# Recurrent layer: head outputs with tokens on partitions, normed by a root for each token, and turned on PE behind the turns of k and v

## What is computed

```python
def hgrn2_mixer(x, w_in, w_out, norm_g, lb):
    H, K, V, C = HGRN_HEADS, HGRN_DK, HGRN_DV, HGRN_CHUNK      # 8, 128, 128, 64
    q_raw, f_raw, i_raw = jnp.split(x @ w_in, [H * K, 2 * H * K], axis=-1)
    log_f = jnp.logaddexp(jnp.log(lb), jnp.log1p(-lb) + jax.nn.log_sigmoid(z))      # z = f_raw
    key, q, v = (1.0 - lb) * jax.nn.sigmoid(-z), jax.nn.silu(q_raw), i_raw
    b = jnp.cumsum(log_f, axis=3)                              # within a chunk
    q_dec, k_dec = q * jnp.exp(b), key * jnp.exp(-b)
    a = jnp.where(causal, jnp.einsum('bhcid,bhcjd->bhcij', q_dec, k_dec), 0.0)
    o_intra = jnp.einsum('bhcij,bhcje->bhcie', a, v)
    # states: the running sum of keys times values, decayed from chunk to chunk
    o = o_intra + jnp.einsum('bhcid,cbhde->bhcie', q_dec, states)
    o = o * lax.rsqrt(jnp.mean(o * o, axis=-1, keepdims=True) + RMS_EPS) * norm_g   # per head and token
    return o.reshape(B, S, H * V) @ w_out
```

## Time and profile before

| | |
|---|---|
| median of 3 runs | 2247.62 us (2245.55 to 2248.52) |
| the profiled execution | 2243.69 us, its span 2241.9 us |
| PE busy | 2137.8 us, 95% of the span |
| DVE busy | 1280.1 us, 57% |
| ACT busy | 886.7 us, 40% |
| mean granted clock of PE | 0.968 of full speed |
| chain that ended last | PE 81%, DVE 11%, DVEq 4%, ACT 2% |

### The profile page before, as it was taken

One profiled execution on the slowest core, in us unless ns is written; L12 is line 12 of the kernel. 1 busy time (PEld: TensorE's weight loads), 2 busy tenths in 40 slices (PEclk: granted clock), 3 DMA queues, 4 the chain that ended last, 5 costly groups with the idle time before them and its releaser, 6 DMA issues.

```text
span 2241.9 us, 29415 instructions
## 1 busy us (share of the span) xinstructions
PE 2137.8 (95%) x11002; PEld 1741.6 (78%) x11002; DVE 1280.1 (57%) x2043; ACT 886.7 (40%) x1298; POOL 69.3 (3%) x63
## 2 busy tenths in 40 slices
PE   7969999999999999999988999999999998999997
PEld 5757778888877888888877788888777876888886
DVE  6987454434454666666676642344568886433444
ACT  4225232222227556566552431242345524322322
POOL 1000300000130000000000000000000000000000
PEclk8988999999999999999999899999999998999998
DMA  4102222232232212212221223222112221222221
GB/s 168 30 10 78 93 75 94 86 114 100 71 117 85 85 59 74 85 66 70 80 76 52 76 97 109 94 94 94 57 58 75 75 76 67 102 94 94 94 96 55
DMA packets 31518, 183.46 MB, mean 82 GB/s; under 512 B 5184, under 2 KB 5568, under 8 KB 12736
## 3 DMA queue, kind: packets, MB, share of 16 engines
q1 hardware_dynamic: 27504, 176.18, 23.1%
q10 hardware_dynamic: 3024, 6.00, 0.8%
q0 software_dynamic: 896, 0.06, 0.0%
HBM read 180.06 MB, written 2.10 MB: 81 GB/s over the span
## 4 chain that ended last, share of the span: by engine, by line
PE 81%; DVE 11%; DVEq 4%; ACT 2%; issue 1%; DMA 1%; ACTq 0%
PE ps L569 12%; PE ps L571 12%; PE ps L570 12%; PE ps L1058 6%; PE ps L1060 5%; PE ps L1059 5%; PE ps L1114 2%; PE ps L1115 2%; PE ps L1116 2%; PE ps L630 1%; PE ps L620 1%; PE ps L599 1%; PE ps L625 1%; PE ps L969 1%; DVE f_run L2608 1%
## 5 line engine op out<-in xcount | busy, mean ns | idle before, releaser
L1284 ACT ACTIVATE w_hi<-raw 128x2048 fp32r<-128x2048 f32 (+1 forms) x122 | 226.0, 1853 | 297.1 <-PE ps L571 220.2
L569 PE MATMUL ps<-x_hi,w_lo 128*128 128x512 f32 x816 | 317.6, 389 | 0.5 <-DVE y L2205 0.3
L571 PE MATMUL ps<-x_hi,w_hi 128*128 128x512 f32 x816 | 317.5, 389 | 0.0
L570 PE MATMUL ps<-x_lo,w_hi 128*128 128x512 f32 x816 | 317.4, 389 | 0.0
L1725 DVE TENSOR_TENSOR w_lo<-raw,w_hi 128x2048 fp32r<-128x2048 f32 (+3 forms) x116 | 259.3, 2235 | 93.1 <-ACT w_hi L1284 92.6
L1058 PE MATMUL ps<-x_hi,w_lo 128*128 128x512 f32 x544 | 218.8, 402 | 2.9 <-DVE w_lo L2375 2.4
L1060 PE MATMUL ps<-x_hi,w_hi 128*128 128x512 f32 x544 | 213.1, 392 | 0.0
L1059 PE MATMUL ps<-x_lo,w_hi 128*128 128x512 f32 x544 | 212.5, 391 | 0.0
L569 PEld LDWEIGHTS ps<-x_hi,w_lo 128*128 128x128 f32 x816 | 153.2, 188 | 32.9 <-issue 0.7
L570 PEld LDWEIGHTS ps<-x_lo,w_hi 128*128 128x128 f32 x816 | 153.2, 188 | 31.9
L571 PEld LDWEIGHTS ps<-x_hi,w_hi 128*128 128x128 f32 x816 | 153.2, 188 | 31.8
(11 more groups left out here) (453 smaller groups left out, 3966.5 us busy)
## 6 DMA issues: line engine op xcount, KB each, us to landing
raw<-w_attn_in SPq DMA_DIRECT2D x32, 1024.0 KB, 5.0
raw<-w_gate_up SPq DMA_DIRECT2D x22, 1024.0 KB, 4.9
raw<-w_up_a SPq DMA_DIRECT2D x16, 1024.0 KB, 4.9
raw<-w_down_a SPq DMA_DIRECT2D x16, 1024.0 KB, 4.9
raw<-w_up_h SPq DMA_DIRECT2D x16, 1024.0 KB, 5.0
raw<-w_down_h SPq DMA_DIRECT2D x16, 1024.0 KB, 4.9
raw<-w_hgrn_in SPq DMA_DIRECT2D x8, 1024.0 KB, 4.9
raw<-w_down SPq DMA_DIRECT2D x8, 768.0 KB, 4.3
```

The source lines that it names most:

```text
L569: pe.matmul(o, w_lo[:, slot, a:a + P], hi[:, k, :], start=k == 0, stop=False)
L570: pe.matmul(o, w_hi[:, slot, a:a + P], lo[:, k, :], start=False, stop=False)
L571: last = pe.matmul(o, w_hi[:, slot, a:a + P], hi[:, k, :], start=False, stop=k == st.kc - 1)
L1284: act.activation(w_hi[:, slot, 0:width], raw[:, slot, 0:width], ACT.Copy).then_inc(whi_ready, 1)
```

## The change

- PE: L1200 and L1208 swap their operands, so that the head's output has tokens on the partitions: four blocks of 128 tokens by 128 features in bank 7, for head 7 too (`O_LAST` goes). The state's part writes one half of the partitions at a time, 64 tokens of a chunk. L1216 goes. New is `turn_head`: four transposes of the scaled output `hg_tok` into bank 5, for head `hd - 2`, behind the turns of k and v; the one of head 7 stands at the end, before the last chunk of the output projection.
- ACT: four squares of 128 columns, each of which also sums over its columns (`accum_out`), give the sum for each token; the root is one of 128x4. The high part `xo_hi` is read from bank 5 with the gain as scale. In step 8 an early root of one element loads the table for it.
- DVE: `scale_head` takes a reciprocal of 128x4 and scales bank 7 into `hg_tok` (128x512), in all steps with an `attend`, at the end of the step. The low part `xo_lo` is read from bank 5 too, with the gain in it.
- The key-value products of head `a` wait for the low part of head `a - 1`, since bank 5 holds its turned output, and no longer for the root.

```diff
             def step(hd, par, project, attend):
 
                 a, old = hd - 1, 1 - par
-                o_bank = O_BANK if project else O_LAST
...
+                if not (isinstance(hd, int) and hd < 2):
+                    turn_head(hd - 2)
                 if project:
                     hgrn_tile(hd, par, 1, range(DC))
                 else:
                     out_part(0, range(4, 5))
                 if attend:
                     pe.wait_ge(ht_ready, a + 1)
-                    pe.wait_ge(root_ready, SK["head0"] + a)
+                    if not first(a):
+                        pe.wait_ge(xlo_ready, XB["hgrn_out"] + a)
...
-                        pe.matmul(ps[:, o_bank, sl], v_htok[:, b, :], tmp[:, 3, sl], start=b == 0, stop=False,
+                        pe.matmul(ps[:, O_BANK, sl], tmp[:, 3, sl], v_htok[:, b, :], start=b == 0, stop=False,
...
-                        sl = slice(c * CHUNK, (c + 1) * CHUNK)
-                        last = pe.matmul(ps[:, o_bank, sl], state[:, c, :], q_dec[:, old, sl], start=False, stop=c == 7,
-                                         skip_group_check=True)
+                        half, at_ = CHUNK * (c % 2), (c // 2) * P
+                        last = pe.matmul(ps[half:half + CHUNK, O_BANK, at_:at_ + P], q_dec[:, old, c * CHUNK:(c + 1) * CHUNK],
+                                         state[:, c, :], start=False, stop=c >= 6, skip_group_check=True)
...
-                    pe.wait_ge(sq_ready, SB["head0"] + a + 1)
-                    pe.matmul(ps[:, 5, :], ones, sq[:, 0, :], start=True, stop=True).then_inc(sq_used, 1)
+
+            def turn_head(n):
+
+                pe.wait_ge(oh_ready, n + 1)
+                for b in range(TB):
+                    last = pe.transpose(ps[:, 5, b * P:(b + 1) * P], hg_tok[:, b, :], ident)
+                last.then_inc(oht_done, 1)
...
             step(HG_HEADS, 0, False, True)
             out_part(1, range(3, 6))
-            out_part(0, range(6, DC))
-            out_part(1, range(6, DC))
-            pe.wait_ge(oh_ready, HG_HEADS)
+            out_part(0, range(6, DC - 1))
+            out_part(1, range(6, DC - 1))
+            turn_head(HG_HEADS - 1)
+            out_part(0, range(DC - 1, DC))
+            out_part(1, range(DC - 1, DC))
...
                 if attend:
                     act.wait_ge(oh_done, a + 1)
-                    act.activation(sq[:, 0, :], ps[:, SUM if project else O_LAST, :], ACT.Square).then_inc(sq_ready, 1)
+                    for b in range(TB):
+                        act.activation(sq[:, 0, b * P:(b + 1) * P], ps[:, SUM, b * P:(b + 1) * P], ACT.Square,
+                                       accum_out=mean4[:, b:b + 1])
...
-                    act.wait_ge(sq_used, SB["head0"] + a + 1)
+                    act.drain()
                     act.wait_ge(rstd_ready, SK_ROOT["head0"] + a)
-                    act.activation(root[:, :], ps[:, 5, :], ACT.Sqrt, bias=eps[:, 0:1], scale=1.0 / P) \
-                       .then_inc(root_ready, 1)
+                    act.activation(root4, mean4, ACT.Sqrt, bias=eps[:, 0:1], scale=1.0 / P).then_inc(root_ready, 1)
...
-            def finish(a, bank):
+            def scale_head(a):
                 dve.wait_ge(root_ready, SK["head0"] + a + 1)
-                dve.reciprocal(rstd[:, :], root[:, :]).then_inc(rstd_ready, 1)
-                settle()
-                stt(chunk(hg_o, a), ps[:, bank, :], gains[:, ds(GAIN_AT["g_hgrn"] + a, 1)], rstd[:, :], ALU.mult,
-                    ALU.mult).then_inc(oh_ready, 1)
+                dve.reciprocal(rstd4, root4).then_inc(rstd_ready, 1)
+                settle()
+                tt(hg_tok[:, :, :], ps[:, SUM, :].rearrange("p (b f) -> p b f", b=TB),
+                   rstd4.unsqueeze(2).to_broadcast([P, TB, P]), ALU.mult).then_inc(oh_ready, 1)
```

More of the change, by code:

```diff
@@ L189, in build @@
     f_start = at("f_start", Y_AT + 2 * KB, [T])
+    hg_tok = at("hg_tok", Y_AT + 4 * KB, [TB, P])
     k_tok = at("k_tok", Y_AT + 12 * KB, [TB, P])
@@ L291, in build @@
         SUMS += [("mean_" + part, 0), ("var_" + part, 8)]
-    SUMS += [(f"head{n}", 1) for n in range(HG_HEADS)]
+    SUMS += [(f"head{n}", 0) for n in range(HG_HEADS)]
     for part in ("mix_h", "ffn_h"):
@@ L393, in build @@
     oh_done, oh_ready = sem("oh_done"), sem("oh_ready")
+    oht_done = sem("oht_done")
     out_done = sem("out_done")
@@ L1195, in step @@
                         out_part(1, range(0, 2))
-                    elif not (isinstance(a, int) and a == 0):
+                    if not first(a):
                         pe.wait_ge(oh_ready, a)
@@ L1679, in step @@
                        .then_inc(ht_ready, 1)
-                if project and not (isinstance(hd, int) and hd < 2):
+                if not (isinstance(hd, int) and hd < 2):
                     head_hi(hd - 2)
@@ L1687, in step @@
                         split_next(hd, par, i, 1)
+                if not project:
+                    act.activation(sq[:, 1, 0:1], eps[:, 0:1], ACT.Sqrt)
                 if attend:
                     act.wait_ge(oh_done, a + 1)
-                    act.activation(sq[:, 0, :], ps[:, SUM if project else O_LAST, :], ACT.Square).then_inc(sq_ready, 1)
+                    for b in range(TB):
+                        act.activation(sq[:, 0, b * P:(b + 1) * P], ps[:, SUM, b * P:(b + 1) * P], ACT.Square,
+                                       accum_out=mean4[:, b:b + 1])
                 if project:
@@ L1694, in step @@
                 if attend:
-                    act.wait_ge(sq_used, SB["head0"] + a + 1)
+                    act.drain()
                     act.wait_ge(rstd_ready, SK_ROOT["head0"] + a)
-                    act.activation(root[:, :], ps[:, 5, :], ACT.Sqrt, bias=eps[:, 0:1], scale=1.0 / P) \
-                       .then_inc(root_ready, 1)
+                    act.activation(root4, mean4, ACT.Sqrt, bias=eps[:, 0:1], scale=1.0 / P).then_inc(root_ready, 1)
             def head_hi(hd):
-                act.wait_ge(oh_ready, hd + 1)
-                act.activation(chunk(xo_hi, hd), chunk(hg_o, hd), ACT.Copy).then_inc(xhi_ready, 1)
+                act.wait_ge(oht_done, hd + 1)
+                act.activation(chunk(xo_hi, hd), ps[:, 5, :], ACT.Copy, scale=gains[:, ds(GAIN_AT["g_hgrn"] + hd, 1)]) \
+                   .then_inc(xhi_ready, 1)
             step(0, 0, 0, True, False)
@@ L1710, in _ @@
             step(HG_HEADS, 0, 0, False, True)
-            head_hi(HG_HEADS - 2)
             head_hi(HG_HEADS - 1)
@@ L2611, in step @@
                     stt(k_dec[:, par, :], hg_k[:, par, :], rest_, f_run[:, :], ALU.mult, ALU.mult).then_inc(dec_ready, 1)
-                if attend and project and not (isinstance(hd, int) and hd == HG_HEADS - 1):
-                    finish(a, SUM)
+                if attend:
+                    scale_head(a)
             step(0, 0, True, False)
```

9 lines of the change are left out of this document (2 added, 7 removed).

## The result

The changed kernel takes 2250.29 us (median of 20 runs, 2247.64 to 2253.66), the kernel before, run beside it, 2245.82 (20 runs, 2238.16 to 2249.13): ratio 1.0023, interval 1.0015 to 1.0031, so 5.2 us slower (3.4 to 7.0) on that median. The profiled execution of the changed kernel took 2250.28 with a span of 2248.5.

What follows compares the result with a forecast made beforehand. The prediction took the recurrent layer's steps as bound by DVE from kv products to k_dec and by PE from there back. Turns +3.0 and end +1.7 made +4.7 us, 2247.6 to 2252.3; range 2248.5 to 2261.

Steps and rivals of the forecast that it cites:

- Two sections with different owners: recurrent layer's step: DVE owns kv products to k_dec, 16.0 us; PE owns k_dec to kv products, 7.5; other's work hidden.
- ones matmul: L1216 on PE, between kv products and k_dec: removal frees 1.0 us a step, worth nothing where DVE is late.
- the shorter passes: L1208's 14 passes on PE, between kv products and k_dec: 1.48 us become 1.0, the saving hidden in the steps.
- The turns: four transposes on PE between k_dec and kv products, steps 2 to 7: 0.5 us each step, +3.0 us.
- The four squarings: ACT's summing squares of 128 columns: at most 3.3 us, making ACT at most 2.7 later, covered.
- rival 4: turns wait for the scaling because the root is late: from 2253 us upward, chance 0.04.
- The reciprocal: on DVE between k_dec and kv products: 3.35 us becomes 0.17, worth nothing as DVE already waits there.
- DVE's slack ahead of the kv products: DVE's total wait for the key-value products in the stage: from 21.3 us to about 45.
- The end: step 8 and the stage's end, where PE's order decides: +1.7 us, bounds 0.5 to 3.3.
- the bound by PE: rival: PE's work bounds the steps, so the kernel gets faster, 2241.8 us; chance 0.07, 0.04 more for a milder form.
- The end that costs nothing: rival: step 8's kv products and the weights' split don't wait; only the turns cost, 2250.3 us, chance 0.13.
- The fall of the clock: rival: PE's clock drops in the longer wait at the scores; two falls 2255.7 us, all seven 2264.2, chance 0.22.

Runs made afterwards that it cites:

- run 1: the changed kernel with the head's four turns of steps 2 to 7 moved behind the kv products: 2248.1 us, ratio 1.0011 to the kernel before.
- run 9: the changed kernel with head 7's turns earlier and the end's chunks in the order of the kernel before: 2246.9 us, ratio 1.0001.
- runs 2 and 3: the changed kernel with unread turns of v added in steps 1 to 8: eight behind the kv products (ratio 1.0015), or four behind the scores (1.0033).
- run 7: the changed kernel with DVE splitting the next weights' low part twice in steps 1 to 7, for longer PE waits: 2275.0 us, ratio 1.0121.
- run 10: the changed kernel with kv products three chunks early, head 7's turns early, v's copy before the squarings, end chunks in before's order: 2236.8 us, ratio 0.9965.
- run 6: the kernel before with the kv products put ahead of the last two chunks of tile 1: 2240.7 us, ratio 0.9973.

## Why the prediction was right

**Two sections with different owners.** This carried the forecast, and runs 1 to 3 show it. The 1.0 us of the ones matmul and the shorter passes (1706.73 - 1705.71 = 1.02, forecast 1.0) moved nothing, and reappear as PE's wait at the scores: 2.6 to 11.2 us, forecast 13. The wait is 1.72 a step, forecast 1.8 to 1.9.

**The turns, +3.0 forecast, +2.2 measured.** Right in place, off in size. They take 0.44 us, with nothing for a wait in front (I had 0.5), so 6 x 0.44 = 2.6. The other 0.4 is the first of these periods: it grew by 0.05 only (23.94 to 23.99), since before lost 0.45 us there in DVE's section, in a gap for which the profile shows no cause. The changed kernel has no such gap in that period, and run 1 has it again (period 23.92), which is why run 1 gave back 2.3 us and not 2.6. DVE in before and in run 1:

```profile
1683.78 3.35 DVE L2608 RECIPROCAL f_run<-f_cum 128x512 f32<-128x512 f32 x1 [0.45 <-issue]
```
```profile
1687.54 0.75 DVE L2630 SCALAR_TENSOR_TENSOR k_dec<-hg_k,lbp,f_run 128x512 f32<-128x512 f32 x1 [0.46 <-issue]
```

What makes such a gap come and go stays open; that it fell this way is luck, and no part of the forecast.

**ACT and DVE.** The four squarings with their sums take 1706.83 to 1707.98, 1.15 us, well within the bound of 3.3; the root ends at 1710.19 and DVE takes it at 1714.72. Covered by 4.5 us, so rival 4 had no ground. The reciprocal went from 3.35 to 0.17 and gave nothing, as forecast. One share was misjudged: of DVE's slack ahead of the kv products I had 45 us in a single wait. It is 34.4 there, and 8.3 in a new wait for ACT's high part in steps 2 to 7 (the rest of that wait's 15.5 is 7.1 for head 7, behind the last kv products, and 0.15 in step 8); in the steps it costs nothing.

**The end, +1.7 forecast, +1.9 measured.** The three waits of the forecast are there: 0.82 for xo_lo ahead of step 8's kv products (forecast 0.7), 1.56 behind the turns where before had 1.49 (forecast 0.1 more), 1.11 for the weights (forecast 1.3, taken from the attention layer's 1.11). Run 9 shows the cause of the last, the order of the chunks. An unforecast wait of 0.83 us at the first chunk of step 8, for the copy of v, where L1216 stood between before, fell ahead of scores that waited 0.93 for k_dec anyway; that is also why the waits at the scores came to 11.2 and not 13.

**The sum.** 4.2 us in the stage against 4.7, the terms off by 0.8 and 0.2 in opposite directions, and 5.2 (3.4 to 7.0) by the ratio. So a part of the closeness is luck. The forecast of the median, 2252.3, is 2.0 above the measured 2250.3, mostly since it started from a median of three runs, 2247.6, that was 1.8 above the one of twenty. Of the rivals, the bound by PE is ruled out by runs 2 and 3. The end that costs nothing is ruled out by the waits of 0.82 and 1.11, neither of which before has there. The fall of the clock did not come, but run 7 shows it was near: with waits 0.4 to 0.7 us longer, and a second one a tile ahead, it came at the scores in 4 steps of 7, at the 1.7 us each that I had given it, and twice at tile 0 behind waits of 1.69 and 1.70. The Trainium skill (TensorE: Matmul & The Clock Gate, Part 4, PE-mode transpose) says that transposes don't count as PE work for the clock gate; twelve turns behind each wait of 1.72 us did not bring a fall here, and no run tells whether they helped to one in run 7.

## What to carry over

Split a pipelined step at the hand-overs between the engines and ask of each edit in which section it lies: the same four turns cost 0.44 us or nothing, and 1.5 us of PE work taken out where another engine is late buys only a longer wait. Such a wait is then the thing to spend: moving 1.4 us of work a step across the hand-over turned it into 9 us, twice what the change itself cost. Where operations at a stage's end are put behind others, look which slot or bank the last of them frees.

## What the runs showed of the hardware

- A wait at a matmul group costs more than its own length: from the first of eight scores passes to the turns it is 0.99 to 1.00 us behind a wait, be it of 0.20 (run 10) or 1.72 us (the changed kernel), and 0.89 in each of run 6's steps, which have none. Over seven steps this is 0.7 of the 1.8 us by which run 6 beat its forecast, and the products behind the mask (0.92 to 0.81) are as much again; the remaining 0.3 or so is not split further.
- Fourteen passes that hold 64 columns and stream 128, alternating between halves of the partitions, take 1.02 us, 0.073 each; with 128 columns held and 64 streamed they took 1.48, 0.106 each.
- The length of a wait in otherwise dense work does not tell by itself whether the clock falls. In the changed kernel it stayed at 1.00 behind six waits of 1.71 to 1.73 us. In run 7 it fell to 0.50 behind waits of 2.12 to 2.46 us at the scores in four steps of four (the scores at 1699.28 ran slow, the matmuls at 1703 at full speed again), and behind one of 2.18 ahead of step 8's first chunk, but behind waits of 1.68 to 1.70 at tile 0 in two of six. What decides there, the wait some 20 us earlier or something else, is open: nothing was changed alone.
